# Retention stage: the ScalarE queue issues each rotation's row swap at the due time of its operand and its slot

## The chip, the cores and the metric

The kernel runs on one core of one Trainium2 chip. Its time is the device time of one execution, in microseconds (us). Before the change it is 3083.76 us, the median of three runs (3080.12 to 3085.23). The profile comes from one more execution of its own.

## The reference, cut to what matters

The program computes two blocks in sequence on 512 tokens of width 1024 (and 256 context tokens in the first). The change lies in the first layer of the second block, `hybrid_ab`. The retention half of that layer takes eight heads of 64 channels:

```
proj = h @ w_in
y, xr, q, k, v, g = split(proj)
xr  = causal_depthwise_conv(xr, conv_w, conv_b)
lru_out = rg_lru(xr, ...) * gelu(y)            # sigmoid gates, then a scan over the tokens
q = rotary(q, pos);  k = rotary(k, pos) * d ** -0.5
s = einsum('id,jd->ij', q, k) * decay, causal  # per head
o = s @ v;  ret = (o - mean(o)) * rsqrt(var(o) + eps)
out = concat([lru_out, ret * silu(g)]) @ w_out
```

## The kernel before

**Layout.** Channels lie on the 128 partitions and tokens in the free dimension. Two heads of 64 channels share one tile of 128 rows and form a pair; there are four pairs, h = 0 to 3. The even and odd channels of a rotation lie on neighbouring partitions. To rotate a tile x of 128x512 float32, the kernel copies every row to its neighbour's partition (the row swap), and then VectorE computes x * cos + swapped * sin in three operations (`rope`, L2388 to L2390).

**The swaps.** There are eight of them, n = 0 to 7: n even is q of pair n // 2, n odd is k. Each is two DMAs of 128 KB (L750), one for the even rows and one for the odd rows, and ScalarE's queue issues both. They land in one of two slots: a piece of `GB_sb` for n even, a piece of `x_sb` for n odd. Ahead of them the queue waits for ScalarE's store of the operand (`d.out`), and, from n = 2, for the second rotation operation of swap n - 2, which reads the slot last (`roped`, L2378). SyncE fetches the tables of cosines and sines (`in_c_ret`, L2257) into two slots of their own; the one of n is asked for once rotation n - 2 has ended.

**The dense work.** TensorE computes twelve weight groups, g0 to g11, as 32 parts (`Dense.matmuls`, L315), in two PSUM banks, 6 and 7, which alternate. A part can start when the part before it in its bank has been stored by ScalarE (L539). Parts 4 to 7 with the earlier ones are the xr groups, parts 8 and 9 are q of pairs 0 and 1, parts 10 and 11 are k of pairs 0 and 1, parts 12 to 19 are v, parts 20 and 21 are q of pairs 2 and 3, parts 22 and 23 are k of pairs 2 and 3, parts 24 to 27 are the gates (with SiLU), and the last four are y. Each weight group is cut into two float16 halves, first by ScalarE (L290), then by VectorE (L300).

**Between the parts** TensorE computes the recurrence's gates (L2302; ScalarE turns them into sigmoids at L2309 and L2310, then exp at L2314, tanh at L2318 and a root at L2322; VectorE computes the scan at L2332 to L2348), and for each pair the scores in four steps j = 0 to 3 (L2402), their products with v (L2433), and a group norm (L2452, L2456). The scores of step j wait until VectorE (L2411) and ScalarE (L2513) have stored those of step j - 1. The norm's last step in VectorE (`gn_close`, L2488, L2489, L2492) waits for ScalarE's store of the gates part of the same number; the first of these stands in VectorE's queue ahead of the score stores of pair 2.

**What sets the order.** Each queue is written out by `weave`: every stream of instructions gives a due time before it puts its instructions down, and the earliest due goes next. A part of n columns is due for 8 * 3 * n / 2400 us, stretched by 182.88 / 122.88. A due time is not a time of the run: it only sets the order in which one engine's queue holds its instructions. The first pair is due at 77.20 (`pair_at`), the others at 89.20, 122.92 and 134.92. ScalarE's swaps were due at 1.0 before `pair_at`, and those of k 2.2 later.

Of the kernel before, what the change touches and what calls it, by code (L numbers as in the profile page):

```python
# [745 lines left out]
def swap_rows(sp, out, x, done):  # L746


    for i in range(2):
        sp.dma_start(out[i:P:2], x[1 - i:P:2]).then_inc(done, 16)  # L750
# [1418 lines left out]
def in_halves(rows):  # L2169
    return rows.rearrange("p (a c) -> p a c", a=2)  # L2170
# [5 lines left out]
def ab_window(nc, m, wt):  # L2176
# [20 lines left out]
    with stage(nc, *(f"ab_{x}" for x in names)) as (block, *sems):  # L2197
# [37 lines left out]
        pair_at = []  # L2235
# [132 lines left out]
        second_rotation = lambda h: 2.2  # L2368
        scores_at = lambda h: pair_at[h] + 7.0

        def swaps(act):
            for n in range(2 * KB):
                h = n // 2
                yield pair_at[h] - 1.0 + second_rotation(h) * (n % 2)
                p = by_group((3 if n % 2 else 2) if h < 2 else (7 if n % 2 else 6))[h % 2]
                act.wait_ge(d.out[p.by], p.nth)
                if n >= 2:
                    act.wait_ge(roped, 3 * (n - 2) + 2)  # L2378
                swap_rows(act, neighbours[n % 2], in_halves(operand(n)), swapped[n % 2])
# [130 lines left out]
        @block.scalar  # L2510
        def _(act):
            weave(norm.squares(act), norm.root(act), head.halves(act), norm.halves(act), first_act(act), convolve_first(act), lru_act(act), lru_halves(act),
                  ret_store(act, 1, lambda o, i: act.activation(o, i, ACT.Copy), st_act), ret_close(act), gn_act(act), swaps(act),  # L2513
                  gn_halves(act), d.split_hi(act), d.stores(act, "act"))
# [1176 lines left out]
```

## Time and profile before

| | |
|---|---|
| time, median of three runs | 3083.76 us (3080.12 to 3085.23) |
| time of the profiled execution | 3088.69 us |
| its span, first to last instruction | 3086.9 us |
| TensorE matmuls busy | 2950.7 us, 96% |
| VectorE busy | 1836.0 us, 59% |
| ScalarE busy | 1310.4 us, 42% |
| mean granted TensorE clock | 0.984 of full speed |
| the stage (1781 to 2008 us of the span): TensorE, VectorE, ScalarE busy | 199.40, 154.62, 101.03 of 227.00 us |

The span starts with the first instruction of the execution and ends with the last; the starts given below are us from its beginning. A row of the timeline begins with the start and the duration of a run of equal instructions; what stands in brackets at its end is how long the engine sat idle ahead of it and what released it. ACTq and SPq are the sequencers of ScalarE and SyncE, where DMAs are issued; they run ahead of their engines.

### The profile page before, as it was taken

The numbers are of one execution on the slowest core, as the hardware profiler recorded it, in microseconds if no ns is written. First come the engines' busy times: TensorE is split into PE (matmuls) and PEld (weight loads), VectorE is DVE, ScalarE is ACT, GpSimd is POOL, SyncE is SP. The second block draws the span as 40 slices with busy tenths as digits, with TensorE's granted clock in tenths as the row PEclk, the third lists the DMA queues.
The fourth block names the chain that finished last, engine by engine and source line by source line (L and its number), as shares of the span: only waits on it lengthen the run. The fifth ranks groups of instructions, "written<-read, shape, count | busy, mean of one in ns | idle before, by whom it ended". The sixth has DMA issues, their size and how long they took to land. (4 is left out here: it accounts for less than half of the span.)

```text
span 3086.9 us, 48857 instructions
## 1 busy us (share of the span) xinstructions
PE 2950.7 (96%) x19588; PEld 1860.2 (60%) x19588; DVE 1836.0 (59%) x3400; ACT 1310.4 (42%) x2743; POOL 35.7 (1%) x108
## 2 busy tenths in 40 slices
PE   7999999999999999999999988999999989999998
PEld 4576867766656466757554454366655666666654
DVE  6337665555534637765665567677734468777744
ACT  3235545443332325455444353444423238744422
POOL 0000000000000000000000000000000001100000
PEclk9999999999999999999999999999999989999999
DMA  8411112211122221122322323223324420023322
GB/s 335 178 59 43 42 62 73 94 68 52 49 105 85 101 86 57 42 90 69 130 82 106 110 95 113 92 83 110 110 94 128 139 74 2 17 94 110 110 94 84
DMA packets 59364, 282.98 MB, mean 92 GB/s; under 512 B 7773, under 2 KB 13533, under 8 KB 38533
## 3 DMA queue, kind: packets, MB, share of 16 engines
q1 hardware_dynamic: 54485, 274.49, 25.6%
q10 hardware_dynamic: 4656, 5.38, 0.5%
q8 instruction: 157, 2.57, 0.3%
q14 instruction: 66, 0.54, 0.1%
HBM read 261.83 MB, written 6.34 MB: 87 GB/s over the span
## 5 line engine op out<-in xcount | busy, mean ns | idle before, releaser
L315 PE MATMUL banks<-h_sb,wsplit_sb 128*128 128x512 f16 (+2 forms) x6528 | 1216.7, 340 | 44.7 <-PEq L86 18.3
L315 PEld LDWEIGHTS banks<-h_sb,wsplit_sb 128*128 128x128 f16 x6528 | 634.0, 99 | 537.5 <-issue 68.5
L315 PE MATMUL banks<-quads,wsplit_sb 128*128 128x512 f16 (+2 forms) x3300 | 587.4, 337 | 4.6 <-PEq L86 4.6
L300 DVE SCALAR_TENSOR_TENSOR wsplit_sb<-ring_sb,wsplit_sb 128x1024 f16<-128x1024 f32 (+2 forms) x356 | 382.5, 1090 | 251.6 <-ACT wsplit_sb L290 249.5
L290 ACT ACTIVATE wsplit_sb<-ring_sb 128x1024 f16<-128x1024 f32 (+2 forms) x356 | 330.1, 944 | 469.0 <-PE banks L315 419.4
L315 PEld LDWEIGHTS banks<-quads,wsplit_sb 128*128 128x128 f16 x3300 | 321.2, 98 | 254.1 <-issue 8.4
L315 PE MATMUL banks<-wsplit_sb,h_sb 128*128 128x256 f16 x2112 | 240.1, 273 | 0.0
L315 PEld LDWEIGHTS banks<-wsplit_sb,h_sb 128*128 128x128 f16 x2112 | 206.2, 98 | 29.5 <-issue 3.8
L2649 PE MATMUL banks<-h_sb,wsplit_sb 128*128 128x512 f16 x864 | 189.4, 379 | 0.0
L539 ACT ACTIVATE quads<-banks 128x256 f32<-128x256 f32 (+2 forms) x174 | 79.8, 461 | 192.3 <-PE banks L315 192.1
L2649 PEld LDWEIGHTS banks<-h_sb,wsplit_sb 128*128 128x128 f16 x864 | 84.4, 98 | 98.2
L1889 ACT ACTIVATE work_sb<-banks 128x512 f32<-128x512 f32 (+1 forms) x80 | 44.2, 553 | 120.6 <-PE banks L1903 88.0
L2534 DVE SCALAR_TENSOR_TENSOR x_sb<-banks,x_sb 128x512 f32<-128x512 f32 (+1 forms) x42 | 23.6, 563 | 101.3 <-PE banks L315 101.3
L386 ACT ACTIVATE work_sb<-x_sb 128x256 f32<-128x256 f32 (+1 forms) x80 | 33.8, 429 | 88.9 <-DVE x_sb L2534 45.2
L1177 DVE TENSOR_REDUCE small_sb<-banks 128x2 f32<-128x1536 f32 (+1 forms) x40 | 61.7, 1542 | 16.4 <-PE banks L623 15.9
L1182 ACT ACTIVATE work_sb<-banks,small_sb 128x768 f32<-128x768 f32 (+1 forms) x80 | 64.3, 811 | 16.0 <-DVE small_sb L1178 15.8
L3266 ACT ACTIVATE work_sb<-work_sb,small_sb 128x128 f32<-128x128 f32 (+3 forms) x128 | 70.2, 552 | 1.7 <-DVE small_sb L3257 1.7
L584 DVE SCALAR_TENSOR_TENSOR work_sb<-work_sb,banks 128x512 f32<-128x512 f32 (+1 forms) x24 | 14.3, 597 | 82.9 <-PE banks L315 82.9
L623 PE MATMUL banks<-quads 64*128 64x256 f32 (+1 forms) x288 | 56.6, 505 | 6.2 <-ACT work_sb L1182 4.6
L3257 DVE CUSTOM_DVE_ANT_0 work_sb<-banks,GB_sb 128x128 f32<-128x128 f32 (+3 forms) x128 | 57.3, 486 | 7.6 <-PE banks L3245 7.2
L3302 ACT ACTIVATE h_sb<-banks 128x128 f32<-128x128 f32 (+3 forms) x128 | 51.3, 427 | 22.1 <-PE banks L3291 22.1
L3291 PE MATMUL banks<-ident_sb,quads 128*128 128x128 f32 x320 | 51.7, 292 | 9.1 <-ACT h_sb L3302 8.0
(398 smaller groups left out, 3637.4 us busy)
## 6 DMA issues: line engine op xcount, KB each, us to landing
ring_sb<-in_w_in SPq DMA_DIRECT2D x52, 1024.0 KB, 4.9
ring_sb<-in_w_ffn SPq DMA_DIRECT2D x44, 1024.0 KB, 4.8
ring_sb<-in_w_merge SPq DMA_DIRECT2D x48, 768.0 KB, 4.4
ring_sb<-in_w_ffn SPq DMA_DIRECT2D x32, 704.0 KB, 4.0
quads<-in_w_mod SPq DMA_DIRECT2D x12, 1024.0 KB, 23.4
x_sb<-in_w_mod SPq DMA_DIRECT2D x12, 1024.0 KB, 7.1
ring_sb<-in_w_ab SPq DMA_DIRECT2D x12, 1024.0 KB, 4.8
ring_sb<-in_w_nsa SPq DMA_DIRECT2D x10, 1024.0 KB, 5.8
```

The source lines that it names most:

```text
L290: act.activation(m.wsplit[:, s, 0, half * n:half * n + n], m.ring[:, s, half * n:half * n + n], ACT.Copy, scale=WSCALE).then_inc(w.hi[s], 1)
L300: dve.scalar_tensor_tensor(m.wsplit[:, s, 1, half * n:half * n + n], m.ring[:, s, half * n:half * n + n], WSCALE, m.wsplit[:, s, 0, half * ...
L315: mm = pe.matmul(p.bank, *p.terms(k, pw, px), start=(p.opens and k == 0 and z == 0), stop=(p.closes and k == p.depth - 1 and z == 2))
L539: return {"act": lambda eng, p: eng.activation(out, p, func, scale=UNSCALE), "dve": lambda eng, p: eng.tensor_scalar(out, p, UNSCALE, None ...
L623: mm = pe.matmul(self.region(u)[:, a:b], lhsT, rhs, start=True, stop=True, skip_group_check=True)
L1177: step(dve.tensor_reduce(mx, reg[:, 0:2 * unit.off].rearrange("p (c k) -> p c k", c=2)[:, :, 0:unit.nk], AX.X, ALU.max))
L1182: act.activation(E[:, u % 2, c * unit.nk:(c + 1) * unit.nk], reg[:, c * unit.off:c * unit.off + unit.nk], ACT.Exp, bias=sm[:, u % 2, 2 + c ...
L2649: mm = pe.matmul(self.m.ps[:, 4 + j, 0:S], self.m.wsplit[:, self.s1, pw, k * GC + j * P:k * GC + (j + 1) * P], part(self.m.h, px, k, 0, S) ...
L3257: dve.tensor_tensor_reduce(E[u % R][:, c, 0:nk], ps[:, 2 * (u % 2) + c, 0:nk], mask[:, S - nk:S], -SCALE64, 3.0e38, ALU.add, ALU.min, x[:, ...
L3266: act.activation(E[u % R][:, c, 0:nk], E[u % R][:, c, 0:nk], ACT.Exp, bias=x[:, 2 + c:3 + c], scale=-1.0, accum_out=x[:, 4 + c:5 + c]).the ...
L3291: out = pe.transpose(ps[:, 4 + c, b * P:(b + 1) * P], W[u % R][:, c, b * P:(b + 1) * P], m.ident[:, :])
L3302: act.activation(WT[u % R][:, c * nk:(c + 1) * nk], ps[:, 4 + c, 0:nk], ACT.Copy).then_inc(copied, 1)
```

## The change

The due time of the swaps in ScalarE's queue is worked out anew. It is 0.6 after the due time of the operand's part (`p.t1`), and from n = 2 not before 3.4 after the rotation that frees the slot (`pair_at[h - 1]`, for k 2.2 more), and in no case later than the old due time. The waits, the two DMAs, the slots and the queues of the other engines stay.

```diff
         def swaps(act):
             for n in range(2 * KB):
                 h = n // 2
-                yield pair_at[h] - 1.0 + second_rotation(h) * (n % 2)
                 p = by_group((3 if n % 2 else 2) if h < 2 else (7 if n % 2 else 6))[h % 2]
+                free_at = pair_at[h - 1] + second_rotation(h - 1) * (n % 2) + 3.4 if n >= 2 else 0.0
+                yield min(max(p.t1 + 0.6, free_at), pair_at[h] - 1.0 + second_rotation(h) * (n % 2))
                 act.wait_ge(d.out[p.by], p.nth)
                 if n >= 2:
                     act.wait_ge(roped, 3 * (n - 2) + 2)
```

Worked out with the due times of the kernel's own planner, the places in ScalarE's queue are these:

| n | due before | due after | new place in ScalarE's queue |
|---|---|---|---|
| 0 | 76.20 | 38.70 | behind the store of part 8 (38.10), ahead of the last pair of gate sigmoids, L2309 and L2310 (38.86) |
| 1 | 78.40 | 53.94 | behind the store of part 10 (53.34), ahead of L290 of g5 (60.96) |
| 2 | 88.20 | 80.60 | behind the store of part 16 (80.01) |
| 3 | 90.40 | 82.80 | right behind n = 2, ahead of the store of part 17 (83.82) and of L2513 of pair 0 (85.20) |
| 4 | 121.92 | 99.66 | behind the store of part 20 (99.06) and L2513 of pair 1, j = 2 (99.20), ahead of j = 3 |
| 5 | 124.12 | 114.90 | behind the store of part 22 (114.30), ahead of L2465 of pair 0 (115.60) |
| 6 | 133.92 | 126.32 | behind L290 of g9 (122.92) |
| 7 | 136.12 | 128.52 | right behind n = 6, ahead of the store of part 24 (129.54) and of L2513 of pair 2 (130.92) |

## Rows read from the trace of the kernel before

**Rows 1.** The waits, TensorE from 1840 to 1985: us in total, times, longest.
```profile
PE banks L2402 <- DVE quads L2390: 8.9, 2, 6.2
```
**Rows 2.** The timeline of ScalarE: start, duration, engine, line, operation.
```profile
1841.66 0.60 ACT L539 ACTIVATE quads<-banks 128x512 f32<-128x512 f32 x1 [2.78 <-PE banks L315]
1842.15 0.68 ACT L2309 ACTIVATE work_sb<-banks,vecs_sb 128x512 f32<-128x512 f32 x1
...
1843.43 1.28 ACT L2314 ACT_TABLE_LOAD   x1
1844.72 2.56 ACT L2314 ACTIVATE quads<-work_sb,gcols_sb 128x512 f32<-128x512 f32 x4
```
**Rows 3.** The timelines of TensorE and VectorE up to the first scores.
```profile
1853.76 5.34 PE L315 MATMUL banks<-h_sb,wsplit_sb 128*128 128x512 f16 x24 [1.78 <-ACT quads L539]
...
1855.70 1.23 DVE L300 SCALAR_TENSOR_TENSOR wsplit_sb<-ring_sb,wsplit_sb 128x1024 f16<-128x1024 f32 x1 [0.64 <-ACT wsplit_sb L290]
...
1880.61 0.69 DVE L2390 TENSOR_TENSOR quads<-quads,GB_sb 128x512 f32<-128x512 f32 x1
...
1881.35 2.08 PE L2402 MATMUL banks<-quads 64*128 64x512 f32 x4 [6.21 <-DVE quads L2390]
```
**Rows 4.** The timeline of ScalarE in a later stage with the same swaps.
```profile
2443.32 1.15 ACTq L750 DMA_DIRECT2D GB_sb<-quads  x2
...
2448.89 0.58 ACT L539 ACTIVATE quads<-banks 128x512 f32<-128x512 f32 x1
2449.50 1.30 ACTq L750 DMA_DIRECT2D x_sb<-quads  x2
2450.84 1.06 ACT L290 ACTIVATE wsplit_sb<-ring_sb 128x1024 f16<-128x1024 f32 x1 [1.37 <-issue]
```
**Rows 5.** The timelines of ScalarE and VectorE around the first scores.
```profile
1872.24 0.38 ACT L539 ACTIVATE quads<-banks 128x256 f32<-128x256 f32 x1 [0.29 <-PE banks L315]
...
1879.88 0.69 DVE L2389 TENSOR_TENSOR GB_sb<-x_sb,quads 128x512 f32<-128x512 f32 x1
...
1883.51 0.60 ACT L2513 ACTIVATE quads<-banks 128x512 f32<-128x512 f32 x1 [8.27 <-PE banks L2402]
```
**Rows 6.** The timeline of VectorE, rotation of n = 2.
```profile
1892.80 0.69 DVE L2388 TENSOR_TENSOR quads<-quads 128x512 f32<-128x512 f32 x1 [3.08 <-DMA GB_sb<-quads]
```
**Rows 7.** The timelines of the three engines around the scores of pair 2.
```profile
1931.88 1.28 ACT L539 ACT_TABLE_LOAD   x1
...
1934.49 0.60 ACT L539 ACTIVATE quads<-banks 128x512 f32<-128x512 f32 x1 [1.33 <-PE banks L315]
...
1936.30 0.69 DVE L2389 TENSOR_TENSOR GB_sb<-x_sb,quads 128x512 f32<-128x512 f32 x1
...
1937.75 0.69 DVE L2488 TENSOR_TENSOR work_sb<-quads,work_sb 128x512 f32<-128x512 f32 x1
...
1937.78 1.13 PE L2402 MATMUL banks<-quads 64*128 64x512 f32 x4 [2.67 <-DVE quads L2390]
...
1939.21 0.69 DVE L2411 COPY quads<-banks 128x512 f32<-128x512 f32 x1
...
1939.95 0.92 PE L2402 MATMUL banks<-quads 64*128 64x384 f32 x4 [0.30 <-DVE quads L2411]
```
**Rows 8.** The timelines of the three engines around pair 3.
```profile
1947.61 0.69 DVE L2388 TENSOR_TENSOR quads<-quads 128x512 f32<-128x512 f32 x1 [3.83 <-DMA GB_sb<-quads]
...
1953.95 0.58 ACT L2442 ACTIVATE quads<-banks 128x512 f32<-128x512 f32 x1
...
1954.59 1.12 PE L2452 MATMUL banks<-quads 128*128 128x512 f32 x2 [1.04 <-ACT quads L2442]
```
**Rows 9.** The DMA issues from 1780 to 2000: size, median us to landing.
```profile
quads<-in_c_ret SPq DMA_DIRECT2D x8, 512.0 KB, 5.7
```
**Rows 10.** Stretches: PE, PEld, DVE, ACT, POOL busy, then TensorE's granted clock, DMA share, GB/s.
```profile
1881.00:1884.00 3.00, 2.65 (x8) 0.96 (x9) 2.83 (x6) 0.49 (x1) 0.00 (x0) 0.50 0.89 345
1884.00:1887.00 3.00, 2.38 (x14) 1.09 (x12) 1.96 (x4) 0.59 (x2) 0.54 (x2) 0.81 0.35 142
1937.00:1940.00 3.00, 1.93 (x9) 0.56 (x9) 2.77 (x4) 1.02 (x2) 0.03 (x1) 1.00 0.83 289
```

## The prediction

> **What bounds the kernel now.** I read the page first: matmuls are busy 96% of the span, VectorE 59%, ScalarE 42%. A change of order in ScalarE's queue can therefore pay or cost only where TensorE stands still. The second view is the waits of TensorE in this stage. One entry holds most of them: the scores wait for the rotations, 8.9 us in two places, and the longer is 6.2 [rows 1]. That looks like the target of the change, so the question is what ended those two waits, and the timelines answer it.
>
> Pair 0 first. TensorE stands 6.21 us until 1881.35, and the rotation's last operation runs from 1880.61 to 1881.30 [rows 3]. From 1855.70 on, VectorE's timeline has no gap at all up to there: the scan, the cut of the weights and the two rotations follow one another. The swaps are not what the rotation waits for. What started this unbroken run is ScalarE: at 1855.70 VectorE had waited 0.64 us for L290, and TensorE at 1853.76 had waited 1.78 us for ScalarE's store of part 9 [rows 3]. ScalarE itself works without a gap from 1841.66 on, through the sigmoids, exp, tanh and roots with their table loads [rows 2]. So the first wait is set by a chain that begins in ScalarE's queue at 1842.
>
> Pair 2 next. TensorE stands 2.67 us until 1937.78, again straight behind the rotation, whose second operation ends at 1936.99 [rows 7]. VectorE is busy throughout the 19 us ahead of it, and its rotations begin without a wait for a DMA.
>
> Only pairs 1 and 3 show a rotation that waits for its swap: 3.08 us at 1892.80 [rows 6], 3.83 us at 1947.61 [rows 8]. Behind the first TensorE runs through: it has no wait in the stage between 1886 and 1935. Behind the second there is one, 1.04 us at 1954.59, for L2442 [rows 8].
>
> **The change part by part.** No instruction is added or taken away; sixteen DMAs move in ScalarE's queue, and with them eight waits.
>
> *Swap 0* moves between the store of part 8 and the last gate sigmoids. There it waits for the store just ahead of it, which ends at 1841.66 + 0.60 = 1842.26. In the later stage the same sequence stands in the trace: a store ends at 2448.89 + 0.58 = 2449.47, the two issues begin at 2449.50 (0.03 later), take 1.30 us, and the next ScalarE instruction starts 0.04 us after them, having lost 1.37 us to "issue" [rows 4]. A swap into `GB_sb` takes 1.15 us there [rows 4]. So L2309, which started at 1842.15 [rows 2], starts at 1842.26 + 0.03 + 1.15 + 0.04 = 1843.48: 1.33 us later. ScalarE has no gap in which to lose this; L290 and the stores of parts 9 and 10 slip by 1.33, and so does VectorE's run that starts at 1855.70 [rows 3]. TensorE's wait at 1853.76 grows from 1.78 to 3.11, which the wait of 6.21 behind it takes in, but that wait too ends 1.33 later, because VectorE does. Cost **+1.33**. Bounds: 0 if the issues overlapped ScalarE's work as they did at their old place, 1.37 + 0.11 = 1.48 by the analogous idle time, with the overlap added that two neighbouring instructions have without issues between them (L2309 began at 1842.15, before the store's end at 1842.26 [rows 2]).
>
> [...]
>
> *Swap 1* moves behind the store of part 10. It waits for that store and issues for 1.30 us, and the next in the queue, L290 of g5, waits for TensorE anyway: over 3 us before, the same after. 0.
>
> *Swaps 2 and 3* come to stand ahead of the stores of parts 17 to 19 and of pair 0's score stores. Swap 3 waits for the second operation of rotation 1, which ends at 1879.88 + 0.69 = 1880.57 [rows 5], so ScalarE stands still from the store of part 16 at 1872.24 [rows 5] to 1880.57 + 0.03 + 1.30 = 1881.90. What waits behind it: the store of part 17, whose bank is needed by part 19 long after, and L2513, which could start at 1883.51 before [rows 5]; the store in between ends at about 1882.3. Cost 0 with 1.2 us of cover (all of these times move by the same 1.33). Were that cover gone, each us past it would delay the second step of the scores. In return the rotation of n = 2 starts when VectorE is free, 3.08 us earlier [rows 6]. TensorE does not wait there, so the gain is 0; its bound is -3.08, if it shortened the run of TensorE in a way that the trace doesn't show.
>
> *Swap 4* stands behind the store of part 20 and has over 2 us until the next score store; *swap 5* stands behind part 22 and ends 0.2 us before L2465 is released. 0 for both, and no gain: rotations 4 and 5 did not wait for them.
>
> *Swaps 6 and 7* are the costly ones. They stand ahead of the store of part 24. Swap 7 waits for the second operation of rotation 5, to 1936.99 [rows 7]; its issues end at 1936.99 + 0.03 + 1.30 = 1938.32. The store of part 24, done at 1935.09 before [rows 7], now comes behind that, with the table load for SiLU ahead of it (1.28 us, and 0.01 to the next instruction [rows 2, 7]). Before, this load ran at 1931.88, while the store waited for its matmuls. So: 1938.32 + 1.29 = 1939.61, the store ends at 1940.21. This is the wait that takes a place on the path: L2488 in VectorE's queue wants the gates of part 24, and the score copy L2411 stands behind L2488 and L2489. Before, L2488 began at 1937.75 and L2411 at 1939.21, 1.46 us later [rows 7]. After: L2411 from 1941.67 to 1942.36, and TensorE's second step of the scores, 0.05 us after that copy, at 1942.41 where it was 1939.95 [rows 7]. Cost **+2.46**. Bounds: 1.17 if the table load is placed ahead of the swaps (the store then ends 1938.92), and 2.46 + 0.95 = 3.41 if TensorE's clock falls (below).
>
> The page "ScalarE: Activation LUTs" of the Trainium skill, section "What ACT_TABLE_LOAD costs", adds a drain of about 1380 ns to the load's 1283 ns at every switch. By that an estimated 1.38 us would come on top here, 2.46 + 1.38 = 3.84 in place of 2.46. The trace disagrees at the load of 1843.43: 1.28 us, and the next instruction starts at 1844.72, 0.01 after it [rows 2].
>
> *Pair 3* gets back the 1.04 us of its wait [rows 8]. Rotation 6 no longer waits 3.83 us; it starts behind the last score copy, which slips by 2.46, so it ends 1.4 us earlier than before and L2442 with it is ready before TensorE, itself 2.46 later, gets there. Its tables don't take over: the one of n = 7 is asked for at the end of rotation 5, about 1937.7, and lands in 5.7 us [rows 9], ahead of 1946. Gain **-1.04**; bounds 0 and -1.04.
>
> **The sum**: 1.33 + 2.46 - 1.04 = +2.75 us. It was made against an execution of 3088.69 us (span 3086.9), so that one would take 3091.4. The median of the runs lies 4.93 us below the profiled execution, and nothing ties that difference to this stage, so the same +2.75 goes on the median: 3083.76 + 2.75 = **3086.5**.
>
> **The rivals.**
>
> *No cost that can be seen.* Swap 0 slips into ScalarE's run for nothing and the table load goes ahead of the swaps: 0 + 1.17 - 1.04 = +0.1, 3083.9 us. For it: at their old place the issues did run beside ScalarE's activations. Against it: there the operand's store was long done, here it is the instruction just ahead, as in rows 4. Chance 0.20.
>
> *Faster: the swap waits were on the path.* If the 3.08 and 3.83 us that VectorE no longer waits [rows 6, 8] reach TensorE in full, the time is 3083.76 - 6.91 = 3076.9; if only the first does, 3080.7. It decides from the point where TensorE would wait for VectorE's next cut of weights after each rotation; the trace shows no such wait between 1886 and 1935. Chance 0.06, half of it beyond 0.2%.
>
> *Slower: the clock falls in pair 2.* After the 6.21 us wait the granted clock is 0.50 over 1881 to 1884 and 0.81 over 1884 to 1887, that is 1.2 GHz for some 3 + 3 * 0.19 / 0.5 = 4.1 us, and the first four score matmuls take 2.08 us; after the 2.67 us wait it stays at 1.00, and the same four take 1.13 [rows 3, 7, 10]. With the change the wait of 2.67 is followed, after 1.93 us of work [rows 10], by one of 0.30 + 2.46 = 2.76. Should the clock fall there, the four matmuls and their like lose 0.95 and the stretch in all up to 4.1 / 2 = 2.1: 3083.76 + 2.75 + 2.1 = 3088.6, and with no gain in pair 3, 3089.7. A longer hold of the stores than I see (a DMA issue that drags on, in both blocks) would carry it past 3090. Chance 0.16.
>
> *The forecast*, +1 to +4: chance 0.58. That the swaps don't issue earlier is excluded, since the order in the queue is written out; that they don't run earlier holds for rotations 0, 1, 4 and 5, and is in the sum.
>
> **How the numbers follow.** What a measurement of this kernel can tell from no change is 0.2%, 6.2 us; the forecast and the first rival lie inside it. Faster beyond it: 0.03. Slower beyond it (above 3089.9): part of the third rival, 0.07. Within it: 0.90. The range runs from 3080.2 (the first rival's +0.1, less the spread of the three runs below their median, 3.6) to 3091.2 (the clock's case without the gain of pair 3, and the 1.5 by which runs lie above their median).
>
> **What would show it.** Right: two issues on ScalarE's queue at about 1842.3, L2309 1.3 us later, TensorE's scores of pair 0 at about 1882.7 behind a wait of still 6.2 us; no wait of the rotations for `GB_sb` or `x_sb` in pairs 1 and 3; ScalarE idle from 1873 to 1882; in pair 2 the table load behind the issues at about 1939.6 (each with 1.33 added), a second wait of TensorE near 2.8 us for L2411, and none for L2442 in pair 3. Wrong: L2309 where it was, or the table load ahead of swap 6, or a granted clock below 1.00 in pair 2, or scores of pair 0 that start earlier than before.

## The result, and the profile after

The changed kernel takes 3095.40 us, the median of five runs (3093.28 to 3098.44), against 3084.84 for the kernel before: a ratio of 1.0036 with a 95% interval of 1.0021 to 1.0050. A second comparison on another occasion gave 1.0030 (1.0017 to 1.0042). The change makes the kernel slower by 5 to 15 us. Three executions on record, one of the changed kernel, one of the kernel before and one of placed_later2, took 14263.75, 4050.7 and 9837.36 us and are left out of all ratios. The direction was forecast; the size was not: 3086.5 was predicted, and 3091.2 was the top of the range.

The work is the same; the page of the kernel after, busy time by engine:

```profile
PE 2953.8 (96%) x19588; PEld 1859.8 (60%) x19588; DVE 1836.1 (59%) x3400; ACT 1310.6 (42%) x2743; POOL 37.5 (1%) x108
```

The waits of TensorE in the stage, 1838 to 1990 us, which answer to [rows 1]:

```profile
PE banks L2403 <- DVE quads L2391: 5.9, 2, 3.3
PE banks L2403 <- DVE quads L2412: 3.7, 2, 3.1
PE banks L315 <- ACT quads L539: 3.1, 1, 3.1
```

The wait for the rotations fell from 8.9 to 5.9 us, which looks like a gain and is none: TensorE came to it later. Two other waits took its place, for the score copy (L2412; 0.9 us of this kind before) and for ScalarE's store of part 9 (L539; 1.8 before). All lines below the diff are one higher than before.

The place of swap 0 in ScalarE's timeline, against [rows 2]:

```profile
1839.91 0.60 ACT L539 ACTIVATE quads<-banks 128x512 f32<-128x512 f32 x1 [2.78 <-PE banks L315]
1840.53 1.18 ACTq L750 DMA_DIRECT2D GB_sb<-quads  x2
1841.76 0.69 ACT L2309 ACTIVATE work_sb<-banks,vecs_sb 128x512 f32<-128x512 f32 x1 [1.25 <-issue]
```

The gate sigmoid starts 1.85 us after the store's start, where it was 0.49: 1.36 us later. TensorE and VectorE, against [rows 3]:

```profile
1853.38 8.29 PE L315 MATMUL banks<-h_sb,wsplit_sb 128*128 128x512 f16 x24 [3.15 <-ACT quads L539]
...
1880.97 2.08 PE L2403 MATMUL banks<-quads 64*128 64x512 f32 x4 [3.26 <-DVE quads L2391]
...
1885.06 1.65 PE L2403 MATMUL banks<-quads 64*128 64x384 f32 x4 [0.62 <-DVE quads L2412]
...
1888.04 1.22 PE L2403 MATMUL banks<-quads 64*128 64x256 f32 x4
```

Here is what the forecast did not have. The 24 matmuls behind the widened wait take 8.29 us where they took 5.34. That costs nothing, since TensorE waits for the rotations behind them anyway (3.26 us now, 6.21 before). But the second and third step of pair 0's scores take 1.65 and 1.22 us, where the kernel before took 0.92 and 0.70 for the same matmuls. The granted clock is the column ahead of the DMA share, after the engines' busy times; first the kernel after, then the kernel before:

```profile
1855.00:1859.00 4.00, 4.00 (x11) 0.50 0.40 88
1885.00:1889.00 4.00, 3.94 (x14) 0.50 0.12 44
1945.00:1948.00 3.00, 3.00 (x9) 0.50 0.04 17
```
```profile
1855.00:1859.00 4.00, 4.00 (x20) 1.00 0.30 47
1885.00:1889.00 4.00, 3.55 (x25) 0.98 0.08 34
```

At 0.50 the engine runs at 1.2 GHz, and 11 matmuls fit where 20 did. Pair 2, all three engines, against [rows 7]:

```profile
1938.21 0.69 DVE L2390 TENSOR_TENSOR GB_sb<-x_sb,quads 128x512 f32<-128x512 f32 x1
...
1938.99 1.29 ACTq L750 DMA_DIRECT2D x_sb<-quads  x2
...
1939.68 1.13 PE L2403 MATMUL banks<-quads 64*128 64x512 f32 x4 [2.66 <-DVE quads L2391]
...
1940.36 1.28 ACT L539 ACT_TABLE_LOAD   x1 [6.59 <-DVE quads L2391]
1941.65 0.60 ACT L539 ACTIVATE quads<-banks 128x512 f32<-128x512 f32 x1
...
1942.45 0.69 DVE L2489 TENSOR_TENSOR work_sb<-quads,work_sb 128x512 f32<-128x512 f32 x1 [2.82 <-ACT quads L539]
...
1943.90 0.69 DVE L2412 COPY quads<-banks 128x512 f32<-128x512 f32 x1
...
1944.64 1.63 PE L2403 MATMUL banks<-quads 64*128 64x384 f32 x4 [3.08 <-DVE quads L2412]
```

The chain of the prediction stands there link by link: rotation, issues of swap 7, table load, store of the gates, norm, score copy, TensorE. The next score matmuls again take 1.63 us in place of 0.92. In pair 3 the wait of [rows 8] is gone; TensorE starts L2453 with no wait ahead of it:

```profile
1949.95 0.68 DVE L2389 TENSOR_TENSOR quads<-quads 128x512 f32<-128x512 f32 x1
...
1959.64 1.02 PE L2453 MATMUL banks<-quads 128*128 128x512 f32 x2
```

Behind the same widened wait the slow matmuls of part 11 do not always last as long: 8.29, 6.71 and 8.26 us in the three profiles of the changed kernel. The scores of pair 0 start 27.6 us after that wait in all three.

**The account.** I measure one stretch in every profile: from the start of the last four gate matmuls (L2302; 1839.02 before, 1837.27 after) to the start of the last norm matmuls of the second kind (L2456, now L2457; 1977.22 and 1982.18). It went from 138.20 to 144.91 us, +6.71:

| piece, between starts of TensorE's matmuls | before | after | difference |
|---|---|---|---|
| last gate matmuls to part 11's wait ended | 14.74 | 16.11 | +1.37 |
| from there to the scores of pair 0 | 27.59 | 27.59 | 0 |
| scores of pair 0 to its products with v | 10.26 | 12.55 | +2.29 (clock) |
| scores of pair 2, first to second step | 2.17 | 4.96 | +2.79 |
| second step to the products with v | 6.13 | 7.70 | +1.57 (clock) |
| from there to the norm (L2452) | 8.51 | 7.30 | -1.21 |
| all the rest | | | -0.10 |

### The profile page after: what moved, and what is told of

Its sections match the earlier page's. It is cut to its first block and busy times, and to the rows that moved or that the text cites. A ratio compares the mean times of both kernels' runs of the same rounds, so it can differ in the third digit from the quotient of the medians.

```text
span 3091.8 us, 48857 instructions
## 1 busy us (share of the span) xinstructions
PE 2953.8 (96%) x19588; PEld 1859.8 (60%) x19588; DVE 1836.1 (59%) x3400; ACT 1310.6 (42%) x2743; POOL 37.5 (1%) x108
## 5 line engine op out<-in xcount | busy, mean ns | idle before, releaser
L290 ACT ACTIVATE wsplit_sb<-ring_sb 128x1024 f16<-128x1024 f32 (+2 forms) x356 | 330.1, 944 | 471.2 <-PE banks L315 420.8
L539 ACT ACTIVATE quads<-banks 128x256 f32<-128x256 f32 (+2 forms) x174 | 79.8, 461 | 195.1 <-PE banks L315 188.4
```

Source lines behind the costliest of these rows:

```text
L290: act.activation(m.wsplit[:, s, 0, half * n:half * n + n], m.ring[:, s, half * n:half * n + n], ACT.Copy, scale=WSCALE).then_inc(w.hi[s], 1)
L539: return {"act": lambda eng, p: eng.activation(out, p, func, scale=UNSCALE), "dve": lambda eng, p: eng.tensor_scalar(out, p, UNSCALE, None ...
```

## The experiments

Each kernel's stretch comes from its own profile; ratios are of whole times, to the kernel before on the same occasion. base_b to base_d are the kernel before again, after_again and after_c the changed kernel. Kernels without a ratio were executed once, for the profile. "Second score step" is the time of its four matmuls, 0.92 us at full clock.

| kernel | stretch, us | second score step, pair 0 / pair 2 | ratio (95%) |
|---|---|---|---|
| before, base_b, base_c, base_d | 138.20, 138.91, 138.73, 138.56 | 0.92 / 0.92 in all | |
| after, after_again, after_c | 144.91, 145.04, 144.89 | 1.65 / 1.63, 1.53, 1.65 | 1.0036, 1.0030 |
| only0, only0_b | 142.26, 142.29 | 1.65 / 0.92 | 1.0006 (0.9997 to 1.0015) |
| only67, only67_b | 141.26, 141.22 | 0.92 / 1.42, 1.32 | 1.0019 (1.0009 to 1.0028) |
| only1to5 | 139.01 | 0.92 / 0.92 | 1.0001 (0.9992 to 1.0010) |
| linger | 142.88 | 1.65 / 0.92 | 1.0016 (1.0008 to 1.0025) |
| after_fill | 141.04 | 0.92 / 0.92 | 1.0016 (1.0007 to 1.0025) |
| only0_fill11 | 142.58 | 1.65 / 0.92 | |
| only67_table | 142.25 | 1.65 / 1.65 | |
| placed | 136.88 | 0.92 / 0.92 | 0.9997 (0.9989 to 1.0006) |
| placed_fill | 138.46 | 1.55 / 0.92 | 1.0008 (0.9999 to 1.0018) |
| placed_later4 | 139.72 | 1.34 / 1.02 | 0.9999 (0.9991 to 1.0008) |
| placed_later2 | 138.52 | 0.92 / 1.65 | 0.9993 (0.9984 to 1.0001) |

**The parts, one at a time.** The due times of some swaps are new and those of the others old:

```diff
-                yield min(max(p.t1 + 0.6, free_at), pair_at[h] - 1.0 + second_rotation(h) * (n % 2))
+                soon = min(max(p.t1 + 0.6, free_at), pair_at[h] - 1.0 + second_rotation(h) * (n % 2))
+                yield soon if n == 0 else pair_at[h] - 1.0 + second_rotation(h) * (n % 2)    # only0
+                yield soon if n >= 6 else pair_at[h] - 1.0 + second_rotation(h) * (n % 2)    # only67
+                yield soon if 1 <= n <= 5 else pair_at[h] - 1.0 + second_rotation(h) * (n % 2)    # only1to5
```

after_again:

> The changed kernel once more, beside its parts. Theory (order plus clock): slower than before by the 6.7 us that the stage lost in its trace: 1.37 for swap 0, 2.3 of half clock in pair 0's scores, 2.8 for the scores of pair 2, 1.6 of half clock behind them, 1.2 given back in pair 3. Rival (the difference of the medians, 10.6 us, is real and has a second source outside the stage): slower by 9 us or more in this shared comparison too.

Ratio 1.0030; stretch 145.04. The interval, 5 to 13 us, takes in both the 6.7 of the trace and the rival's 9, and its middle, 9.3 us, lies on the rival's side. This run does not decide between them; the 4 us are taken up again below.

only0:

> Only swap 0 is moved. Theory: the issue time slips into ScalarE's unbroken run, TensorE's wait for part 9 grows to 3.1 us, the clock falls behind it and again lasts into the scores of pair 0: +1.4 +2.3 = +3.7 us. Rival (only the issue time counts, the clock in pair 0 is low anyway after the wait): +1.4 us.

only67:

> Only swaps 6 and 7 are moved. Theory: +2.8 for the score copy behind the gates' store, +1.6 of half clock behind the two waits of TensorE, -1.2 in pair 3: +3.2 us. Rival (the clock falls in pair 2 only because pair 0's was low for longer before it): +1.6 us.

only1to5:

> Swaps 1 to 5 are moved, 0, 6 and 7 stay. Theory: rotation 2 starts 3 us earlier on VectorE and nobody waits for it: 0 us, within 0.5. Rival (ScalarE's queue held from 1874 to 1882 delays score stores): +1 us or more. Second rival (the earlier rotations reach TensorE): -1 to -3 us.

Against the mean of four profiles of the kernel before, 138.60, the parts cost +3.7 (swap 0), +2.6 (swaps 6 and 7) and +0.4, sum 6.7; the whole change costs +6.4 (144.95, mean of three). So the parts add up in the stretch, and swaps 1 to 5 are free: the +0.4 of only1to5 is the wait ahead of pair 3's norm, 1.84 us there and 1.04 to 1.73 in the profiles of before. The whole times agree less well: only67 is 5.9 us slower (2.8 to 8.6), only0 1.9 us (-0.9 to 4.6). Each costly part is a slip plus a spell of half clock, as the theory had it. The rival that pair 2's clock falls only because pair 0's did is out: in only67 pair 0 is at 0.92 and pair 2 at 1.42.

**Is it the queue's time or the DMAs?** linger leaves every swap where it was and puts two copies of ScalarE into that place:

```diff
+        def linger(act):
+            yield xr[-1].t1 + 8.22
+            p = by_group(2)[0]
+            act.wait_ge(d.out[p.by], p.nth)
+            for i in range(2):
+                act.activation(ps[:, 5, :], m.x[:, 0, 0:S], ACT.Copy).then_inc(lingered, 1)
+                act.wait_ge(lingered, i + 1)
```

> The kernel before, with two idle ScalarE copies of a tile into an unused PSUM bank in the place where swap 0 went, each waited for: some 1.3 us of the queue and no DMA moved. Theory (the time in ScalarE's run is what counts, and the wait that it widens lets the clock fall): the same as with swap 0 moved alone, 4.1 us more from the last gate matmuls to the last norm matmuls than the 138.2 us before, scores of pair 0 at half clock in their second and third step. Rival (the early transfer of swap 0, or its landing slot, is what disturbs): +1.4 us or less.

TensorE's timeline in linger:

```profile
1855.17 8.25 PE L315 MATMUL banks<-h_sb,wsplit_sb 128*128 128x512 f16 x24 [3.19 <-ACT quads L539]
...
1882.77 2.08 PE L2410 MATMUL banks<-quads 64*128 64x512 f32 x4 [3.30 <-DVE quads L2398]
...
1886.86 1.65 PE L2410 MATMUL banks<-quads 64*128 64x384 f32 x4 [0.62 <-DVE quads L2419]
```

Without a DMA moved, the wait (3.19), the slow part 11 (8.25) and the slow score step (1.65) are all there, and the stretch is 4.3 us over the mean of before, where only0 has 3.7. What swap 0 costs is 1.3 us of ScalarE's queue in its unbroken run.

**Is the rest the clock?** after_fill puts matmuls that nobody reads into TensorE's waits, into the unused PSUM bank 5, with operands that lie still in this stage:

```diff
+        def filler(pe):
+            for at, n in ((53.2, 12), (scores_at(0) - 0.05, 24), (scores_at(2) - 0.05, 10), (scores_at(2) + 0.95, 11)):
+                yield at
+                for i in range(n):
+                    pe.matmul(ps[:, 5, :], part(m.h, 0, i % KD, 0, P), part(m.h, 0, i % KD, 0, S), start=True, stop=True)
```

> The changed kernel, with matmuls that nobody reads, into an unused PSUM bank, in TensorE's four waits: 12 ahead of part 11, 24 ahead of the scores of pair 0, 10 and 11 around the first scores of pair 2. Theory (beside the two slips of 1.4 and 2.8 the loss is TensorE's clock at 1.2 GHz behind the waits): the clock stays at 1.00, the same stretch takes 138.2 + 1.4 + 2.8 - 1.2 - 1.6 (the half clock that the kernel before has too) = 139.6 us, some 5.3 us below the changed kernel. Rival (the clock falls for another reason, or is low by itself): 145 us, or more by the filling.

TensorE's timeline in after_fill:

```profile
1849.53 5.34 PE L315 MATMUL banks<-h_sb,wsplit_sb 128*128 128x512 f16 x24 [0.56 <-ACT quads L539]
...
1870.75 5.34 PE L2410 MATMUL banks<-h_sb 128*128 128x512 f16 x24
1877.11 1.13 PE L2403 MATMUL banks<-quads 64*128 64x512 f32 x4 [1.02 <-DVE quads L2391]
...
1881.21 0.92 PE L2403 MATMUL banks<-quads 64*128 64x384 f32 x4 [2.20 <-DVE quads L2418]
...
1938.49 0.92 PE L2403 MATMUL banks<-quads 64*128 64x384 f32 x4 [0.71 <-DVE quads L2418]
```

With the clock kept at 1.00 throughout, the stretch is 141.04, 3.87 us below the changed kernel, and 2.29 + 1.57 = 3.86 is what the account puts down to the clock. What is left over before is the two slips and the gain: 1.37 + 2.79 - 1.21 = 2.95 against 141.04 - 138.20 = 2.84 (2.44 against the mean of before). The expectation was 1.4 us too low, for an instructive reason: it credited 1.6 us for the half clock that the kernel before has in its first score step (2.08 us for four matmuls). That credit doesn't exist. The first step is now 1.13, and TensorE then waits 2.20 for the score copy in place of 0.62, because the copy stands behind the recurrence's operations in VectorE's queue and starts 3.35 us after the scores do, in the changed kernel as in after_fill. A slow TensorE in front of a late partner costs nothing.

**Does the earlier fall cause the later one?** only0_fill11 is only0 with the 12 filling matmuls ahead of part 11 alone:

```diff
+            for at, n in ((53.2, 12),):
```

> Swap 0 moved alone, and 12 matmuls that nobody reads in the wait ahead of part 11 only. Theory: with that wait filled the clock stays at 1.00 through part 11, TensorE again waits 6.2 us ahead of the scores of pair 0, and the clock is back by their second step as before: 138.2 + 1.4 + 0.4 = 140.0 us for the stretch, the half clock of 2.3 us is gone. Rival (the half clock in the scores' second and third step comes from when the scores start, not from the earlier fall): 142.3 us, as with swap 0 alone.

TensorE's timeline in only0_fill11:

```profile
1854.64 5.34 PE L315 MATMUL banks<-h_sb,wsplit_sb 128*128 128x512 f16 x24 [0.56 <-ACT quads L539]
...
1882.22 2.08 PE L2404 MATMUL banks<-quads 64*128 64x512 f32 x4 [6.20 <-DVE quads L2392]
...
1886.31 1.65 PE L2404 MATMUL banks<-quads 64*128 64x384 f32 x4 [0.62 <-DVE quads L2419]
```

The theory fell. Part 11 runs at full clock, the wait ahead of the scores is 6.20 as before, and the second step is slow all the same: 142.58, as the rival said. What differs is when the clock falls. TensorE and the granted clock in the 3 us ahead of the scores, the 4 us from their start and the 3 us after, first the kernel before, then only0_fill11:

```profile
1878.35:1881.35 3.00, 0.00 (x0) 0.50 0.84 238
1881.35:1885.35 4.00, 3.47 (x10) 0.53 0.78 316
1885.35:1888.35 3.00, 2.90 (x20) 1.00 0.08 34
```
```profile
1879.22:1882.22 3.00, 0.00 (x0) 0.82 0.85 266
1882.22:1886.22 4.00, 3.47 (x10) 0.50 0.76 309
1886.22:1889.22 3.00, 2.91 (x10) 0.50 0.03 11
```

In the kernel before, the clock is down for the whole of the last 3 us of the wait and back before the second step. In only0_fill11 it falls 1.1 us ahead of the scores (0.82 is 1.9 us at full clock and 1.1 at half) and stays down through the second and third step.

**The table load.** only67_table is only67 with one SiLU of a single column ahead of swap 6:

```diff
+                if n == 6:
+                    act.activation(m.gcols[:, 94:95], m.ones[:, 0:1], ACT.Silu)
```

> Swaps 6 and 7 moved alone, with one SiLU of a single column ahead of swap 6, so that its table is loaded before the swaps' waits. Theory (1.28 us of the 2.8 is the table load behind the swaps): TensorE's wait for the second score step is 1.8 us where it was 3.08, and the clock keeps; the stretch takes 138.2 + 1.5 - 1.3 = 138.4 us. Rival (the load is not what counts, the store comes as late): 141.3 us.

TensorE's timeline in only67_table:

```profile
1885.27 2.08 PE L2406 MATMUL banks<-quads 64*128 64x512 f32 x4 [6.20 <-DVE quads L2394]
...
1889.36 1.65 PE L2406 MATMUL banks<-quads 64*128 64x384 f32 x4 [0.62 <-DVE quads L2415]
...
1943.57 1.13 PE L2406 MATMUL banks<-quads 64*128 64x512 f32 x4 [2.67 <-DVE quads L2394]
...
1947.26 1.65 PE L2406 MATMUL banks<-quads 64*128 64x384 f32 x4 [1.25 <-DVE quads L2415]
```

First to second step of pair 2 takes 1947.26 - 1943.57 = 3.69 us, where only67 has 4.97 (1936.55 to 1941.52): the load was 1.28 us of the slip, as expected. But the stretch was not 138.4: the clock fell in both pairs. In pair 0, where this kernel is the kernel before, that had not been seen yet. In pair 2 it was down before the second wait: the three matmuls between the first step and that wait took 1.38 us for 0.82, so here the wait of 2.67 alone was enough.

**Does the slow clock of pair 0 belong to the change?** So the kernel before was profiled three more times, and only0 once.

base_b:

> The kernel before, profiled once more. If the long half clock in pair 0's scores belongs to moving swap 0: 138.2 us for the stretch and 0.92 us for the second step's four score matmuls. If it is a matter of the execution: 1.65 us for them and 140.5 us in about half of such profiles.

base_c:

> The kernel before, a third profile, as for base_b: 0.92 us and 138.2 us if the long half clock belongs to the move of swap 0, else 1.65 us and 140.5 us in about half of such profiles.

base_d:

> The kernel before, a fourth profile, as for base_b: 0.92 us and 138.2 us if the long half clock belongs to the move of swap 0, else 1.65 us and 140.5 us in about half of such profiles.

only0_b:

> Swap 0 moved alone, profiled once more. If the long half clock belongs to the move: 1.65 us again for the second step's four score matmuls, 142.3 us for the stretch. If it is a matter of the execution: 0.92 us and 140.0 us as likely as that.

All three profiles of before have 0.92, only0_b has 1.65. Over all profiles without filling matmuls ahead of the scores: where ScalarE's run is widened (after three times, only0 twice, linger, only0_fill11) the second step is slow in 7 of 7; where it isn't, and the scores are where they were (before four times, only67 twice, only1to5, placed, only67_table), in 1 of 9. The slow clock goes with the 1.3 us, if not without exception. What keeps the clock down longer once the stage runs 1.3 us later is not shown.

**The 4 us outside the stage.** After the stretch, the four profiles of before have 1109.7, 1106.3, 1106.5 and 1106.7 us to the end of the span, and kernels with swaps 6 and 7 moved had up to 1115.0.

after_c:

> The changed kernel, profiled a third time. Theory (the stage loses 6.4 us against the mean of four profiles of before, and what comes behind it varies by execution): 145 us for the stretch, and 1106 to 1110 us behind it. Rival (the change also costs clock in the later stages): 1109 us or more behind it again.

only67_b:

> Swaps 6 and 7 moved alone, profiled once more. Theory: 141.3 us for the stretch, and 1106 to 1110 us behind it. Rival (the change also costs clock in the later stages): 1111 us or more behind it again, as in the first profile (1115.0).

Behind the stretch after_c has 1107.1 and only67_b 1107.6 us. The stretches of one kernel repeat within 0.2 us (0.7 for the kernel before), what comes behind varies by 7.4 us with one and the same kernel (only67: 1115.0 and 1107.6). TensorE behind the stretch, in base_b and in only67:

```profile
1977.67:3084.00 1106.33, 1056.98 (x7231) 0.99 0.27 90
1979.06:3094.10 1115.04, 1068.10 (x7231) 0.98 0.27 89
```

The same 7231 matmuls keep TensorE busy for 11.1 us longer at the lower granted clock, so what varies there is the clock too. Spans of the three profiles of after average 3092.8, those of the four of before 3084.9: 8.0 us, of which the stretch has 6.4. The rest is not shown to be the change's, and not excluded either. In the seven profiles with swaps 6 and 7 at the new place it is 1107.1 us or more behind the stretch; in seven of the nine with these swaps at the old place it is 1106.3 to 1106.7, in the other two 1109.7 and 1112.8. And the ratios put the whole loss above that of the stretch for after (11.1 and 9.3 us against 6.4), only67 (5.9 against 2.6) and after_fill (4.9 against 2.4).

**Better places.** placed keeps swaps 0 and 1 at the old due times, takes the new ones for 2 to 5, and puts 6 and 7 behind the store of part 24:

```diff
+                yield (76.2, 78.4, 80.6, 82.8, 99.66, 114.9, 130.0, 130.1)[n]
```

> Swaps 0 and 1 at their old due times, 2 to 5 at the new ones, 6 and 7 behind the store of part 24 (due 130.0), ahead of the score stores of pair 2. Theory (what cost was the place ahead of part 8's followers and of part 24's store, the earlier rotation of pair 3 is worth its wait): TensorE has no wait for L2442, 137.1 us for the stretch, 1.1 us faster than before, within what can be told from none. Rival (swap 7's wait delays the first score store of ScalarE): +1 us or more.

ScalarE's timeline in placed:

```profile
1931.72 1.28 ACT L539 ACT_TABLE_LOAD   x1
1934.34 0.60 ACT L539 ACTIVATE quads<-banks 128x512 f32<-128x512 f32 x1 [1.33 <-PE banks L315]
1934.40 1.15 ACTq L750 DMA_DIRECT2D GB_sb<-quads  x2
1936.92 1.29 ACTq L750 DMA_DIRECT2D x_sb<-quads  x2
1938.82 0.60 ACT L2514 ACTIVATE quads<-banks 128x512 f32<-128x512 f32 x1 [3.88 <-PE banks L2403]
```

The table load and the store are back where they were, swap 7 is issued in the gap ahead of the score store, and pair 3 has no wait. The stretch is the shortest of all, 136.88, 1.7 us below the mean of before. By the two ratios, whose intervals lie apart, it is faster than the changed kernel; from the kernel before, the whole time can't tell it (0.9997, 0.9989 to 1.0006).

placed_fill has the filling matmuls too, 6, 24 and 10 of them at the first three places.

> The same places, with the filling matmuls: 6 ahead of part 11, 24 ahead of the scores of pair 0, 10 ahead of those of pair 2. Theory: the clock of pair 0's scores is kept, 1.6 us less again, 135.5 us, 2.7 us faster than before. Rival (filling matmuls overrun the waits or slow others): slower than the kernel with the same places and no filling.

It missed: 138.46. The filled wait only moved the idleness on: TensorE waits 2.20 for the score copy, and the clock falls there (second step 1.55).

placed_later4 and placed_later2 put off the scores, masks, products and norm of pair 0 in the queues by 4.0 and 2.0:

```diff
-        scores_at = lambda h: pair_at[h] + 7.0
+        put_off = lambda h: 4.0 if h == 0 else 0.0
+        scores_at = lambda h: pair_at[h] + put_off(h) + 7.0
```

> The better places (0 and 1 old, 2 to 5 early, 6 and 7 behind the store of part 24), and the scores, masks, values and norm of pair 0 due 4.0 later, so that TensorE takes the matmuls of v (part 18 and a part of 19) in the wait for the rotations. Theory: 6.2 us of wait take up to 2.7 us of the dense work, the clock keeps: 136.9 - 2.7 = 134.2 us for the stretch, 4 us faster than before. Rival (VectorE's queue, which now holds more of the scan ahead of the score copies, is the bound): 137 us or more.

> The same with 2.0 in place of 4.0. Theory: 1.4 us of dense work in the wait, 135.5 us for the stretch, 2.7 us faster than before. Rival: as above, 137 us.

Both missed, with 139.72 and 138.52. With 4.0, the dense work that was to fill the wait itself waited 5.07 us for a store of ScalarE (L539), which stands behind swap 3, and in pair 2 the clock fell after a wait of 3.12 (1.97 us for the first step). With 2.0 the clock fell in pair 2 (2.08 and 1.65 for the first two steps), at a wait of 2.67 behind which the first step took 1.13 in every other kernel with that wait.

## Why the prediction was right or wrong

**Where the time is lost** was right: TensorE's waits, and the two places in ScalarE's queue. Swaps 1 to 5 cost nothing, and the 3.08 us that VectorE gained in pair 1 reached nobody (only1to5: 1.0001).

**Swap 0, +1.33**: measured +1.37. The pattern taken from the later stage held to 0.04 us. The two issues took 1.18 us, the sum had 1.15.

**Swaps 6 and 7, +2.46**: measured +2.79. The table load came behind the swaps, as taken, and cost 1.28. The page "ScalarE: Activation LUTs" of the Trainium skill, section "What ACT_TABLE_LOAD costs", adds a drain of about 1380 ns to a load of 1283 ns. The load agrees, the drain does not appear: the store starts 0.01 us after the load. The missing 0.33 are hand-overs between engines that I had set too low: 0.09 from the rotation to the issue where I had 0.03, 0.08 from the issue to the table load, and 0.20 from the end of the store (1942.25) to VectorE (1942.45) where I had none.

**Pair 3, -1.04**: measured -1.21 here. The wait was 1.04, 1.73, 1.55 and 1.39 in four profiles of before, so the term, 0.17 more than the wait, is nearer to -1.6; the one profile that I had showed its smallest value. That the three terms together come so near (2.75 forecast, 2.95 measured) is in part luck: with a gain of 1.6 they would make 2.56.

**The step that failed** is the clock. The prediction wrote that the wait at 1853.76 growing to 3.11 is something "which the wait of 6.21 behind it takes in", and its third rival looked for a falling clock in pair 2 alone, with 0.95 to 2.1 us and a chance of 0.16. In the likeliest case the clock term was zero. Measured, it is +2.29 in pair 0 and +1.57 in pair 2, 3.86 us together, more than the two slips less the gain (2.95); after_fill takes it out and leaves 2.84. For pair 2 the mechanism was on the page of rivals with the right size and too small a chance: it came in every profile with that second wait (5 of 5). For pair 0 it was missing. I had taken the score matmuls' clock as given by the length of the wait ahead of them, 6.21 us in both kernels, and in only0_fill11 that very wait, 6.20 us, was followed by the slow steps. The prediction also took the half clock from the start of the scores on, 4.1 us; it had fallen 3 us earlier, inside the wait, and in the kernels in which it fell later it also came back later.

**The range** was made for one loss at a time. The top, 3091.2, is the forecast with the clock's fall in pair 2, no gain in pair 3 and 1.5 us for the spread of the runs. The true sum in the stage, 6.4 to 6.7 us, gives 3083.76 + 6.7 = 3090.5, inside it. The medians, 3095.4 and 3096.8, hold more. With five runs the kernel before is itself at 3084.84, 1.1 above; the other 4 us or so lie outside the stretch, and whether they are the change's or the executions' stays open.

**What stays open**: what makes the clock fall and come back later in pair 0 when the stage runs 1.3 us later there, why one kernel without the move showed it too, and what part of the loss outside the stretch belongs to the change. It was not tried to shift the scores against everything else by small steps.

## What to carry to other kernels

A DMA issued from a compute engine's queue is an instruction with a wait in front of it: price its two issues (1.2 to 1.3 us) and its wait against what stands behind it in that queue, a table load among it, and put it in a gap of the engine, behind the stores that others want. When a change widens a wait of TensorE, put a clock term in the likeliest case and not only in a rival, and read the granted clock behind each of its waits in more than one trace of before. And an operand that arrives earlier is worth only the wait of the engine at the bound behind it: 3.8 us earlier in pair 3 gave 1.2, 3.1 in pair 1 gave nothing.

## What was not expected of the hardware

After a wait of 6.20 to 6.21 us ahead of the same matmuls, TensorE's second score step took 0.92 us in eight profiles and 1.65 in only0_fill11 and only67_table: the length of a wait alone does not say how long 1.2 GHz lasts behind it. In the eight the clock fell 3.0 to 3.2 us ahead of the scores, in these two 1.1 and 2.0 us ahead. A wait of 2.66 followed by one of 3.08, with 1.9 us of work between, brought the clock down in all of five profiles. After a single 2.67 us it came down in placed_later2 and in only67_table, and not in ten other profiles. At its old place, at about 1945 us, the pair of issues of swap 7 took 1.28 to 2.60 us, elsewhere 1.28 to 1.31. The wait of pair 3 is not set by it: in only0_fill11 it took 1.28 us and the wait was still 1.75. That wait goes with the landing of swap 6, for which the rotation waited 3.83 to 4.63 us while the wait of pair 3 went from 1.04 to 1.84.
